# GpSimd takes square sums and some weight remainders; the opening and three orders of work are changed in a two-block transformer kernel

## The reference

```python
def first_block(x, mem, ...):
    x = x + gated_branch_mixer(rmsnorm(x, norm_mix_g), ...)      # 31-tap convolution, pooling, 3-tap convolution
    x = x + memory_cross_attention(rmsnorm(x, norm_x_g), rmsnorm(mem, norm_mem_g), ...)
    x = x + hierarchical_moe(rmsnorm(x, norm_ffn_g), ...)        # 16 experts
    return rmsnorm(x, norm_f_g)

def rmsnorm(x, g):
    xf = x.astype(jnp.float32)
    y = xf * lax.rsqrt(jnp.mean(xf * xf, axis=-1, keepdims=True) + EPS)
    return (y * g.astype(jnp.float32)).astype(x.dtype)

def second_block(x, c, ...):
    for i in range(2):
        mod = silu(c) @ w_ada[i] + b_ada[i]                      # sh1, sc1, g1, sh2, sc2, g2
        x = x + g1 * (nsa_mixer or diff_mixer)(rms_norm(x, ln_mix_g[i]) * (1 + sc1) + sh1)
        h = rms_norm(x, ln_mlp_g[i]) * (1 + sc2) + sh2
        x = x + g2 * (square(relu(h @ w_mlp_in[i])) @ w_mlp_out[i])
```

## Time and profile before

| | us |
|---|---|
| median of 3 runs | 1316.54 |
| lowest and highest | 1315.47, 1316.83 |
| the profiled execution's own time | 1315.27 |
| its span, first to last instruction | 1313.5 |
| PE busy | 1290.3 |
| DVE busy | 950.7 |
| ACT busy | 657.9 |
| GpSimd (POOL) busy | 88.5 |

### The profile page before, as it was taken

How to read it: one execution, slowest core, us unless ns; L and a number is a source line. 1 busy time by engine, 2 the same in 40 slices (tenths; PEclk the granted TensorE clock), 3 DMA queues, 4 the chain that set the end, 5 groups by cost and what they waited for, 6 DMA issues and landing times.

```text
span 1313.5 us, 24511 instructions
## 1 busy us (share of the span) xinstructions
PE 1290.3 (98%) x10581; PEld 1237.9 (94%) x10581; DVE 950.7 (72%) x1199; ACT 657.9 (50%) x872; POOL 88.5 (7%) x134
## 2 busy tenths in 40 slices
PE   7999999999999999999999999999999999999998
PEld 7999999999999999999989689999999888999998
DVE  5769897764797667777776978877789666754443
ACT  4544436364643434343657747454456455654441
POOL 4003000000000000020100000100000020000000
PEclk9999999999999999999999999999999999999999
DMA  9665555545488777885632046999875431465550
GB/s 280 202 206 176 182 176 166 187 135 179 161 288 297 258 258 267 284 284 166 209 128 92 6 161 225 322 313 325 312 235 168 165 97 65 161 192 193 180 174 33
DMA packets 172701, 259.67 MB, mean 198 GB/s; under 512 B 5157, under 2 KB 147794, under 8 KB 172594
## 3 DMA queue, kind: packets, MB, share of 16 engines
q1 hardware_dynamic: 160906, 203.13, 47.1%
q0 software_dynamic: 10848, 53.69, 11.6%
q10 hardware_dynamic: 840, 1.28, 0.3%
HBM read 257.03 MB, written 1.05 MB: 196 GB/s over the span
## 4 chain that ended last, share of the span: by engine, by line
PE 86%; DVE 8%; ACT 3%; issue 2%; DMA 1%; SPq 0%; POOL 0%; ACTq 0%; DVEq 0%
PE ring L675 59%; PE acc L675 24%; ACT w_hi L1503 2%; DVE w_lo L2051 2%; PE acc L1276 1%; DVE arena L2100 1%; PE ring L1085 1%; DMA raw<-in_w_in_dram 1%; ACT h_hi L1503 1%; ACT arena L1503 1%; DMA arena<-in_w_ada_dram 1%; DVE arena L2464 0%; DVE h_lo L2096 0%; DVE h_lo L2094 0%; DVE norm L2066 0%
## 5 line engine op out<-in xcount | busy, mean ns | idle before, releaser
L675 PE MATMUL ring<-h_hi,w_hi 128*128 128x256 f32 (+1 forms) x2016 | 575.0, 285 | 5.7 <-DVE w_lo L2051 1.8
L675 PE MATMUL ring<-h_hi,w_lo 128*128 128x256 f32 (+1 forms) x2016 | 568.2, 282 | 0.0
L675 PE MATMUL ring<-h_lo,w_hi 128*128 128x256 f32 (+1 forms) x2016 | 566.5, 281 | 0.0
L2051 DVE TENSOR_TENSOR w_lo<-raw,w_hi 128x2048 fp32r<-128x2048 f32 x189 | 430.9, 2286 | 165.4 <-ACT w_hi L1503 164.7
L1503 ACT ACTIVATE w_hi<-raw 128x2048 fp32r<-128x2048 f32 x191 | 363.2, 1905 | 132.1 <-PE ring L675 64.0
L675 PEld LDWEIGHTS ring<-h_hi,w_hi 128*128 128x128 f32 x2016 | 379.8, 188 | 11.8 <-issue 7.3
L675 PEld LDWEIGHTS ring<-h_lo,w_hi 128*128 128x128 f32 x2016 | 380.7, 189 | 2.6 <-issue 2.2
L675 PEld LDWEIGHTS ring<-h_hi,w_lo 128*128 128x128 f32 x2016 | 380.9, 189 | 0.0
L675 PE MATMUL acc<-e_hi,w_hi 128*128 128x256 f32 x768 | 216.9, 282 | 2.9 <-DVE e_lo L2752 1.5
L675 PE MATMUL acc<-e_hi,w_lo 128*128 128x256 f32 x768 | 215.1, 280 | 0.0
L675 PE MATMUL acc<-e_lo,w_hi 128*128 128x256 f32 x768 | 215.1, 280 | 0.0
(11 more groups left out here) (317 smaller groups left out, 1348.2 us busy)
## 6 DMA issues: line engine op xcount, KB each, us to landing
arena<-in_w_ada_dram POOLq DMA_DIRECT2D x64, 768.0 KB, 6.3
raw<-in_w_mlp_in_dram SPq DMA_DIRECT2D x32, 1024.0 KB, 5.8
raw<-in_w_mlp_out_dram SPq DMA_DIRECT2D x32, 1024.0 KB, 5.0
raw<-in_w_in_dram SPq DMA_DIRECT2D x24, 1024.0 KB, 5.8
raw<-in_w_e_gate_dram SPq DMA_DIRECT2D x16, 1024.0 KB, 6.3
raw<-in_w_e_up_dram SPq DMA_DIRECT2D x16, 1024.0 KB, 5.4
raw<-in_w_e_down_dram SPq DMA_DIRECT2D x16, 1024.0 KB, 5.0
raw<-in_diff_w_in_dram SPq DMA_DIRECT2D x12, 1024.0 KB, 5.3
```

The source lines that it names most:

```text
L675: return nc.tensor.matmul(dst, lhs, rhs, start=start, stop=stop, **kw)
L2051: tt(w_lo[q % RAW][:, 0:n], raw[q % RAW][:, 0:n], w_hi[q % SPL][:, 0:n].bitcast(F32), ALU.subtract)\
```

## The change

- **Square sums.** GpSimd folds the first three pairs of squares (`fold_two`: pair 0 + pair 1; `fold_rest`: + pair 2, then block 0 + block 1). PE sums the folded block and the two blocks of the last pair, three calls in one place (`stat_sums`), behind block 3 of the raw panel, for d behind block 6. `stat_pair` is gone.
- **Row norm of the memory.** ACT squares the rows with an accumulator, takes the root; DVE inverts it and scales the rows; only then does PE turn them, and DVE multiplies with the gain as it takes them from PSUM. `stats("mem")` and `scaled` are gone.
- **Opening.** The gain of the first norm is loaded ahead under its own semaphore and turned alone. DVE makes the norm's first two products ahead of remainder 0 and copies the other vectors behind panel 1. Panel 1 is split and multiplied in two halves (`two_halves`). SP loads panel 2 ahead of the memory.
- **Orders.** In the MoE `ahead(PN["moe"] + 1)` moves forward on DVE and ACT, and the second ada piece behind the first act. In the MLP `chunk_lo(1)` stands ahead of `ada(1, 4)`.
- **Remainders.** Those of panels 5, 8, 11, 14, 18, 21, 24, 27, 30, 33, 36 and 39 are made by GpSimd, four ahead of the window sums, eight behind. They count on a semaphore of their own.

Some semaphores are shared under new names; that changes no order.

```diff
+        POOL_LO = (5, 8, 11, 14, 18, 21, 24, 27, 30, 33, 36, 39)
+        def by_dve(p):
+            return p - sum(q < p for q in POOL_LO)
...
             load_panel(sp, turn, 1)
-            sp.wait_ge(S("vecs_landed"), 16 * N_VEC_DMA)
+            sp.wait_ge(S("vecs_landed"), 16 * (N_VEC_DMA - 1))
+            load_panel(sp, turn, 2)
             m_rows = a["mem"][0].rearrange("(t p) n -> p t n", p=P)
...
+            def remainder(q, sem):
+                pool.wait_ge(S("hi_made"), q + 1)
+                nc.gpsimd.tensor_tensor(w_lo[q % RAW][:], raw[q % RAW][:], w_hi[q % SPL][:].bitcast(F32), ALU.subtract)\
+                    .then_inc(S(sem), 1)
+            for q in POOL_LO[:4]:
+                remainder(q, "pool_split")
             W = T + 16
...
+            def fold_two(tag):
+                pool.wait_ge(*sig(tag + "_squared", 2))
+                nc.gpsimd.tensor_tensor(sq[:, 0:2], sq[:, 0:2], sq[:, 2:4], ALU.add).then_inc(S(tag + "_folded"), 1)
+            def fold_rest(tag):
+                pool.wait_ge(*sig(tag + "_squared", 3))
+                pool.wait_ge(*sig(tag + "_folded", 1))
+                nc.gpsimd.tensor_tensor(sq[:, 0:2], sq[:, 0:2], sq[:, 4:6], ALU.add).then_inc(S(tag + "_folded"), 1)
+                pool.wait_ge(*sig(tag + "_folded", 2))
+                nc.gpsimd.tensor_tensor(sq[:, 0], sq[:, 0], sq[:, 1], ALU.add).then_inc(S(tag + "_folded"), 1)
...
                 for n in range(ADA_FIRST):
                     ada_load(turn, l, n, at(n))
+                    if n == (1, 3)[l]:
+                        fold_two(("ffn", "m0")[l])
+                        if l == 0:
+                            fold_rest("ffn")
+                if l == 1:
+                    fold_rest("m0")
...
+            for q in POOL_LO[4:]:
+                remainder(q, "pool_split")
+            fold_two("x")
+            fold_rest("x")
...
+            def stat_sums(tag):
+                f, sq = FL[tag + "_stat"], blk(SQX, 8)
+                open_fill(f)
+                pe.wait_ge(*sig(tag + "_folded", 3))
+                mm(bank(f)[:, 0:T], ones[:], sq[:, 0], True, False)
+                pe.wait_ge(*sig(tag + "_squared", 4))
+                mm(bank(f)[:, 0:T], ones[:], sq[:, 6], False, False)
+                mm(bank(f)[:, 0:T], ones[:], sq[:, 7], False, True).then_inc(S(tag + "_summed"), 1)
...
-            full("a_gate", split="mix_ready", together=1)
-            pe.wait_ge(S("mem_landed"), 16)
+            linear_first([PN["a_gate"]], FL["a_gate"], block_ready("mix_ready"))
+            two_halves(PN["a_gate"] + 1, FL["a_gate"] + 1)
+            pe.wait_ge(S("mem_rows"), 2)
             turn_rows(lambda i: acc[i], 2048, "mem_turned")
             full("a_val")
-            stats("mem", lambda k: blk(SQ + k)[:, 0], "mem_squared")
...
+            act.wait_ge(S("mix_ready"), KB)
+            act.wait_ge(S("mem_landed"), 16)
+            for t in range(2):
+                last = func(blk(SQ + 4 * t, 4), arena[:, 2048 + t * D:2048 + (t + 1) * D].rearrange("p (b t) -> p b t", b=4),
+                            ACT.Square, accum_out=stat[:, 4 + t:5 + t])
+            last.then_inc(S("mem_squared"), 1)
+            act.wait_ge(S("mem_squared"), 1)
+            func(stat[:, 6:8], stat[:, 4:6], ACT.Sqrt, scale=1.0 / D, bias=eps[:]).then_inc(S("mem_squared"), 1)
             ahead(0)
...
+            dve.wait_ge(S("mem_squared"), 2)
+            chain.did(nc.vector.reciprocal(stat[:, 6:8], stat[:, 6:8]))
+            chain.settle()
+            for t in range(2):
+                rows = arena[:, 2048 + t * D:2048 + (t + 1) * D]
+                ts(rows, rows, stat[:, 6 + t:7 + t], None, ALU.mult).then_inc(S("mem_rows"), 1)
             ahead(0)
...
+            ahead(PN["moe"] + 1)
             dve.wait_ge(S("cond_made"), 1)
-            for n in range(2):
-                ada(0, n)
+            ada(0, 0)
...
             tt(act0, act0, row, ALU.mult).then_inc(S("act_made"), 1)
-            ahead(PN["moe"] + 1)
+            ada(0, 1)
             expert_lo(0)
...
                 ahead(PN[name] + 1)
+                chunk_lo(1)
                 if l == 0:
                     ada(1, 4)
-                chunk_lo(1)
```

More of the change, by code:

```diff
@@ L534, in _ @@
             loads(sp, turn)
-            p = 2
+            p = 3
             while p < len(plan):
@@ L660, in _ @@
             ada_loads(1)
+            fold_two("d")
+            fold_rest("d")
             for q in (PN["d_o"], PN["d_o"] + 1):
[L663 to L666, removed]
+                pool.wait_ge(S("panel_split"), by_dve(q))
+                remainder(q, "panel_split")
+            fold_two("m1")
+            fold_rest("m1")
         @block.tensor
@@ L688, in open_panel @@
             def open_panel(p):
-                pe.wait_ge(S("panel_split"), turn.at("panel", p + 1))
+                if p in POOL_LO:
+                    pe.wait_ge(S("pool_split"), POOL_LO.index(p) + 1)
+                else:
+                    pe.wait_ge(S("panel_split"), by_dve(p) + 1)
             def linear(p, f, nk, nb, hi, lo, ready=None, dst=None):
@@ L748, in raw_first @@
                         last.then_inc(S("moe_input_used"), 1)
-                    for j in sums.get(k, ()):
-                        stat_pair(tag, j)
+                    if k == sums:
+                        stat_sums(tag)
             def raw_next(tag, p, dst):
@@ L2073, in sums_wait, with split_norm @@
                     dve.wait_ge(S("panel_done"), p + 1)
-            def scaled(tag, src, dst, gain, nb=KB):
-                inverse(tag)
-                chain.settle()
-                for b in range(nb):
-                    last = stt(dst(b), src(b), gain(b), norm[:, 2, :], ALU.mult, ALU.mult)
-                    if b % 2:
-                        last.then_inc(S(tag + "_scaled"), 1)
-            def split_norm(tag, gain, shift=None, mid=SQX, row=None):
+            def split_norm(tag, gain, shift=None, mid=SQX, row=None, behind_two=None):
                 if row is None:
@@ L2165, in _ @@
                stat[:, 2:4].unsqueeze(2).to_broadcast([P, 2, P]), ALU.mult).then_inc(S("mix_diagonal"), 1)
-            ahead(1 - SPL)
+            dve.wait_ge(S("mix_gain_turned"), 1)
+            drains(nc.vector.tensor_copy(mix_gain[:], bank(FL["mix_gain"])[:, 0:KB]), FL["mix_gain"])
+            dve.wait_ge(S("mix_spread"), 1)
+            chain.did(nc.vector.tensor_copy(norm[:, 2, :], acc[0][:, 0:T]))
+            drained_wait(dve, FL["x_t"] + 3)
+            drained_wait(dve, FL["mix_gain"])
+            split_norm("mix", lambda b: mix_gain[:, b:b + 1], mid=SQ, row=2, behind_two=lambda: ahead(1 - SPL))
+            for b, sem, split in ((0, "first_half_hi", "first_half_split"), (1, "hi_made", "panel_split")):
+                c = slice(b * P, (b + 1) * P)
+                dve.wait_ge(S(sem), b + 1)
+                tt(w_lo[1][:].rearrange("p (k n) -> p k n", k=KB)[:, :, c], raw[1][:].rearrange("p (k n) -> p k n", k=KB)[:, :, c],
+                   w_hi[1][:].bitcast(F32).rearrange("p (k n) -> p k n", k=KB)[:, :, c], ALU.subtract).then_inc(S(split), 1)
+            made["lo"] += 1
             dve.wait_ge(S("vecs_turned"), 1)
@@ L2170, in _ @@
             chain.did(last)
-            chain.did(nc.vector.tensor_copy(norm[:, 2, :], acc[0][:, 0:T]))
-            drained_wait(dve, FL["x_t"] + 3)
-            split_norm("mix", lambda b: vcol("mix_g", b), mid=SQ, row=2)
+            dve.wait_ge(S("mem_squared"), 2)
[4 more added lines that the diff above has]
+                ts(rows, rows, stat[:, 6 + t:7 + t], None, ALU.mult).then_inc(S("mem_rows"), 1)
             ahead(0)
```

105 lines of the change are left out of this document (64 added, 41 removed).

## The result

The changed kernel takes 1334.31 us (median of four, 1330.57 to 1335.06) against 1316.43: the ratio is 1.0133, 95% interval 1.0121 to 1.0145. Forecast were 1318.0, range 1309 to 1324. The sign of the likeliest sum was right, the size was not. The profiled execution has a span of 1333.3 against 1313.5, 19.8 more.

What follows compares the result with a forecast made beforehand. PE, busy 98% of the span, was taken as the bound. Terms -3.4 + 7.1 + 3.6 - 2.2 - 2.2 - 0.4 - 0.3 - 1.6 + 0.9 = +1.5 on 1315.27, plus 1.27 to the median: 1318.0, range 1309 to 1324.

Steps and rivals of the forecast that it cites:

- opening to a_val: Start of the kernel: PE's earlier first matmul is lost waiting for the memory's rows; a_val at 33.9 against 34.0, 0.
- convolution: From the gates to the convolution's sum: GpSimd remainders hold DVE's taps and low parts, PE waits until 200, +7.1.
- m0: Norm m0: fold holds DVE's low parts, +1.4; low part ahead of the ada piece ends a wait; net -0.3.
- merges: Ahead of w_o: remainder 39 on GpSimd holds the last add and both low parts, PE goes on at 246.3, +3.6.
- hold of 4.3: Each remainder on GpSimd can hold DVE's taps or low parts for 4.3 us, while saving DVE 2.2.
- first sign that was asked for: DVE taps or low parts of over 4 us beside each GpSimd remainder.
- Rivals 1 and 2: Shorter holds of 3.2, 1313.1, 20%; no hold by long instructions, about -13, 1303, 10%.
- rival 3: Slower: each GpSimd remainder holds DVE for all 4.6; convolution stage 8.7, merges 3.9, 1319.9; 25%.
- wait of 2.7 in x_k's middle: GpSimd's remainder 27 comes after two of the memory's four low parts, so PE waits 2.7 more during x_k.
- walk to 199.9: DVE's convolution end, 191.7 before: low parts 5.9 later, remainder 27 gone (-2.2), remainder 30 holds 4.3; end 199.9.
- Rival 4: Opening: the memory lands a panel (4.1) later than order of issue gives; rows and panel 2's high part go back; 1322, 12%.
- The fifth piece is issued later: 0: Second layer's fifth ada piece, behind the folds on GpSimd's queue: DVE wants it only behind raw panels and norm, 0.

Runs made afterwards that it cites:

- e3: Changed kernel with six extra dummy products (12 PE instructions) at each of five PE waits; 1328.07 us, 1.0091 of the kernel before.
- e4: Changed kernel with m0's ada piece back ahead of the second chunk's low part; 1328.25 us, 1.0104 of the kernel before.
- e6: Changed kernel with all remainders by DVE, m0's ada piece first, only x and ffn folded; 1311.01 us, 0.9960 of the kernel before.
- e11: As e6, with DVE's order in the MoE as before and ACT's kept as changed; 1309.75 us, 0.9960 of the kernel before.
- e9: Changed kernel with m0's ada piece first and only remainder 39 on GpSimd, folds kept; 1317.25 us, 1.0014 of the kernel before.
- e5: Changed kernel with all remainders by DVE and m0's ada piece first, folds kept; 1314.77 us, 0.9988 of the kernel before.
- e8: Changed kernel with m0's ada piece first, only remainders 5, 8, 11, 14, 33 and 36 on GpSimd; 1314.56 us, 0.9988 of the kernel before.
- e2: Kernel before with only the twelve mixer remainders moved to GpSimd; 1325.48 us, 1.0088 of the kernel before.

## Why the prediction was wrong

The sum by its own steps, predicted and measured (differences between columns of the table, row "changed"):

```
opening to a_val   0      +1.2        MoE              -0.4    +0.9
memory's sums     -3.4    -3.4        NSA stage         0      +2.9
convolution       +7.1    +9.5        m0               -0.3    +0.8
merges            +3.6    +4.9        ada piece         0      +5.9
x                 -2.2    -2.2        d                -1.6    +0.5
ffn               -2.2    -2.1        m1               +0.9    +1.0
```

The missed 18.3 (19.8 between the two spans, 1.5 forecast) have one main step behind them (6.1), a second (4.5 beside the clock), and smaller ones.

- **The step that failed** is the pricing of a wait. "PE goes on at 246.3: +3.6" and "PE waits until 200" took a wait's price to be its length. The waits themselves came as forecast: at x_k 3.6 and at w_o 4.2 (3 and near 4 forecast), ahead of the convolution's sum 3.9 (3 forecast), for m0's operands 3.3 (2 to 3, for the last square). But behind each the clock was at half, and PE fell back further while it worked: 1.7 behind the memory's rows, 1.5 at x_k, 1.7 at the sum, 1.3 at w_o, 1.4 at the ada piece. e3 shows it by filling the waits. Without x_k's, which the next wait swallowed, that is 6.1 of the 18.3 that were missed. The clock stood at nothing in the sum.
- **The hold of 4.3** was right. Beside a remainder 12 taps took 9.20 where 12 free of it take 4.84, 16 took 10.76 instead of 6.42 and 20 took 12.39 instead of 8.01: 4.36, 4.34 and 4.38. These lines of the changed kernel are the first sign that was asked for, the third stands above (the last line is the kernel before's sixteen):

```profile
113.36 9.20 DVE L2306 SCALAR_TENSOR_TENSOR arena<-arena,vec 128x256 f32<-128x256 f32 x12
178.79 4.84 DVE L2306 SCALAR_TENSOR_TENSOR arena<-arena,vec 128x256 f32<-128x256 f32 x12
165.92 10.76 DVE L2306 SCALAR_TENSOR_TENSOR arena<-arena,vec 128x256 f32<-128x256 f32 x16
```

```profile
168.18 6.42 DVE L2230 SCALAR_TENSOR_TENSOR arena<-arena,vec 128x256 f32<-128x256 f32 x16
```

 Rivals 1 and 2 fall by them, and rival 3 (4.6) too. The wait of 2.7 in x_k's middle did not come: the four low parts were through before GpSimd, which had to wait, and its hold fell on the taps behind them instead. With the clock's 1.7 taken off, the convolution cost 7.8 and the merges 3.6: 7.1 and 3.6 were forecast. (The walk to 199.9 adds up to 199.7 by its own terms, 191.7 + 5.9 - 2.2 + 4.3, which changes nothing.) At w_o the hold fell on the add, as said, here in the changed kernel and then in the kernel before:

```profile
248.62 4.31 DVE L2376 TENSOR_TENSOR arena<-arena 128x512 f32<-128x512 f32 x1
```

```profile
241.41 0.69 DVE L2300 TENSOR_TENSOR arena<-arena 128x512 f32<-128x512 f32 x1
```

- **The opening** went as walked: the memory's rows were scaled at 31.5 (31.2 forecast), and the memory landed last of the two at 27.3:

```profile
27.37 1.06 ACT L1557 ACTIVATE arena<-arena 128x1024 f32<-128x1024 f32 x1 [5.46 <-DMA arena<-in_mem_dram]
30.12 1.42 DVE L2250 TENSOR_SCALAR arena<-arena,stat 128x1024 f32<-128x1024 f32 x2
```

 a_val then started 1.2 late by the clock alone, which took 1.7 behind the wait. That the landing fell so near the forecast is in part luck: in the kernels run here that load the memory behind panel 2, ACT began its squares between 24.9 and 27.4, and a_val moved with it from 2.2 ahead to 1.2 behind. Rival 4 (a panel later) did not come.
- **"The fifth piece is issued later: 0"** is the second step that failed. Undoing the swap of the piece and the low part was enough to end the wait (e4), with the folds left in GpSimd's queue. The swap's price was counted in DVE's order alone, and the load that DVE's piece releases was not followed to its queue. That is 4.5 of wait besides the clock, shown by e4.
- **d's fold** was given 0.6 of hold; its three folds made two low parts take 1.91 instead of 0.87 and four take 2.72 instead of 1.67, together 2.1 in DVE's chain, and PE's gain went with it: +0.5 where -1.6 stood. m0 is 1.1 worse and m1 as forecast; e6 takes all three folds out at once, and the columns tell them apart.
- **The MoE's order** was priced at -0.4 and measured +0.9. This too is an ada piece whose load follows a panel's (see e11): the piece that was moved on DVE moved its load, and that was again not followed.
- **The NSA stage** is most likely not the change's. In its small products PE runs at half clock in the kernel before too, for about 3.5 us; in the changed kernel for some 10 (clock 0.50 from 716 to 724), in e9 not at all. From 400 to 740 the kernels run here, at unlike moments, moved by -1.7 to +2.9 against the kernel before. These go with the length of the half clock: 10.2 us of it in the changed kernel against 3.4 before is 3.4 us of work lost at half rate, and +2.9 was measured; e9 has none and gains 1.7. What sets that length was not found, and one profile of a kernel can't tell it from chance.
- **The memory's sums, x, ffn and m1** came within 0.1. For x that is luck. The reason given was one remainder less on DVE; in fact the fold was worth its 2.2 only where PE came late enough for the last squares, behind the wait at w_o (changed, e4, e9). Without that wait it brought nothing (e5, e6).

## What to carry to other kernels

On a kernel that TensorE bounds, price a wait by its length and by what its clock does behind it: look at the granted clock and the count of matmuls in the stretch, since a busy share shows neither. Moving a product from VectorE to an idle GpSimd cost nothing only where VectorE's results weren't wanted soon, and it brought nothing there either (e8); where it stopped VectorE's two-input work, it lost 4.4 to save 2.2. When an instruction moves, follow the load that its end releases: one that fell 0.25 us behind another queue's megabyte took 7.8 instead of 4.6.

## What the runs showed of the hardware

- A fallen clock doesn't follow the length of a wait alone. In these traces every wait of 2.9 and more behind the first matmuls had 0.50 at its end or behind it. In e5 (and e9) a wait of 1.94 in m1 was followed by it, in the changed kernel one of 1.95 at the same place was not (e5, then the changed kernel):

```profile
1122.00:1124.00 2.00, 2.00 (x10) 2.00 (x10) 2.00 (x6) 1.45 (x1) 0.00 (x0) 0.50 0.95 336
```

```profile
1142.00:1144.00 2.00, 1.66 (x13) 1.67 (x14) 2.00 (x5) 2.00 (x4) 0.78 (x1) 1.00 0.96 310
```

 and in e3 2.8 at the convolution's sum, behind the dummies, kept 1.00. Two waits of 2.0 for the memory's rows went both ways, down in e4 and not in e5.
- A long GpSimd product that comes in the midst of a train of DVE taps waits for the whole train, not for one tap: it took 11.59 in e2 (20 taps) and 8.38 in the changed kernel (12 taps, which took 4.83 as if alone). It gets in where DVE's train ends or behind a long product, and then DVE waits 4.4. The Trainium skill's page "SBUF — State Buffer", section "Who interferes with whom", has the exclusion and that the order of issue decides who blocks; both are seen here, the wait for a whole train goes beyond it, and GpSimd's short products of 0.80 did take turns with taps in the kernel before.
